# Seven block products for eight in the up projections of a two-layer decoder trunk

## The chip, the cores and the metric

One NeuronCore of a Trainium2 chip runs the whole program. The metric is the device time of one execution in microseconds (us). The engines that matter are TensorE (PE; its weight loads are listed as PEld), VectorE (DVE), ScalarE (ACT), GpSimd (POOL) and SyncE (SP), which issues the loads.

## The reference

The trunk has two layers on 528 tokens (16 meta tokens ahead of 512), of width 1024: a state-space mixer, then differential attention. Behind each mixer stands a gated feed-forward part with a short causal convolution, and this part is what the change touches.

```python
def conv_ffn(h, w_up, conv_w, conv_b, w_down):      # w_up 1024 x 5632, w_down 2816 x 1024
    up = h @ w_up                                    # h: RMS-normalised, with gain
    up_p = jnp.pad(up, ((0, 0), (2, 0), (0, 0)))
    c = conv_b + sum(conv_w[j] * up_p[:, j:j + L] for j in range(3))
    gate, val = jnp.split(c, 2, axis=-1)
    return (jax.nn.silu(gate) * val) @ w_down
```

All arrays are float32.

## The kernel before

**Layout.** Activations lie transposed: channel on the 128 partitions, token along the row. hT holds the residual in 8 channel tiles of 528 tokens. The tokens of a projection are cut into two spans (ALL: 2 x 264 in layer 0; FROM12: 2 x 258 in layer 1), one PSUM bank each.

**Precision.** Each float32 operand is split into a rounded high part and a remainder (wH and wL for weights, hgH and hgL for the input), and three products (high by high, high by low, low by high) are added up in PSUM. The weights come in "units" of 8 k-tiles by 128 columns (1024 elements a partition). load_unit (line 287) has SyncE bring a unit to one of two slots of raw, split_hi (292) has ScalarE write wH, split_lo (299) has GpSimd subtract and write wL. wH and wL have four slots. unit_products (304) issues a unit's 8 x 3 x 2 = 48 matmuls, all of them under line 314.

**Up projection.** The 2816 gate columns and 2816 value columns make 22 pairs (FT = 22) of a gate tile and a value tile: 44 units a layer, 96 matmuls a pair. The gain is applied on the way to hgH and hgL; the row scale rstd is applied afterwards, when VectorE drains the PSUM banks into u (lines 1796, 1797). The sum of squares behind rstd is made by stat_products (line 854), ScalarE takes the root (1391), VectorE the reciprocal (1787). In TensorE's order these statistics stand inside the third unit.

**Convolution.** For each pair VectorE does two tensor_scalar operations, the first taps (1801), and four scalar_tensor_tensor operations, the later taps (1807). ScalarE applies silu to the gate half cg (1402), VectorE multiplies cg by cv (1814). ScalarE then rounds the product into actH (1404), and VectorE writes the remainder actL (1816). A loop of 11 turns with two pairs each drives every engine; the Chain helper (link) puts a semaphore between dependent VectorE operations.

**Down projection.** In layer 0, eight output tiles with three units each again use unit_products, from actH and actL, and VectorE adds the result to hT. In layer 1, down_by_token (line 937) has 24 matmuls of 512 columns for each of the 22 activation tiles and ends in the output norm.

The order within each engine is the order of the code; engines meet only through semaphores.

## Time and profile before

| | us |
|---|---|
| median of 3 runs | 1274.59 (1274.38 to 1275.67) |
| span of the profiled execution | 1273.0 |
| TensorE busy | 1243.4 (98%) |
| VectorE busy | 751.6 (59%) |
| ScalarE busy | 570.7 (45%) |
| GpSimd busy | 607.4 (48%) |
| products of line 314, share of the chain that ended last | 49% |

The span is the time from the first to the last instruction of one execution, on which all rows below were taken. "Busy" is the time in which an engine had at least one instruction recorded. A recorded duration can contain time in which the instruction was held up inside its engine. "Idle before, releaser" names what ended the wait ahead of an instruction.

### The profile page before, as it was taken

What the parts mean: (1) busy time and instruction counts of PE and PEld (TensorE: products, weight loads), DVE (VectorE), ACT (ScalarE), POOL (GpSimd) and SP (SyncE); (2) the same over time, 40 slices, a digit from 0 to 9 for tenths busy, and PEclk for the clock granted to TensorE, in tenths of its full rate; (3) what the DMA queues carried; (4) which work ended last, traced back from release to release, by engine and by line L of the source; (5) the groups of instructions that cost most, each with busy time, mean ns of one, the idle gap of its engine ahead of it and who ended that gap; (6) DMA issues with size and microseconds to landing.
All of it is one profiled execution on the core that took longest, in us unless ns stands there. A gap on an engine that the chain in (4) does not pass through costs nothing.

```text
span 1273.0 us, 26292 instructions
## 1 busy us (share of the span) xinstructions
PE 1243.4 (98%) x10335; PEld 1185.3 (93%) x10335; DVE 751.6 (59%) x1028; ACT 570.7 (45%) x957; POOL 607.4 (48%) x361
## 2 busy tenths in 40 slices
PE   5899999999999999999999999999999999999998
PEld 5888999999999999999998988989999999998886
DVE  8997122688888884111455555553688888882002
ACT  7996543343343432222656656633243333432113
POOL 5433566444444345656654544419544344444431
PEclk9999999999999999999999999999999999999999
DMA  8333332223322333333222112113323333233231
GB/s 174 67 72 82 102 100 84 75 75 99 99 82 87 95 95 91 93 91 112 70 69 65 50 51 68 34 50 100 97 71 97 99 96 86 82 99 99 99 99 66
DMA packets 179498, 108.88 MB, mean 86 GB/s; under 512 B 7100, under 2 KB 173789, under 8 KB 179165
## 3 DMA queue, kind: packets, MB, share of 16 engines
q1 hardware_dynamic: 178997, 107.31, 30.0%
q8 instruction: 51, 0.84, 0.3%
q10 hardware_dynamic: 432, 0.59, 0.1%
q14 instruction: 18, 0.15, 0.0%
HBM read 101.59 MB, written 2.10 MB: 81 GB/s over the span
## 4 chain that ended last, share of the span: by engine, by line
PE 86%; issue 6%; POOL 4%; DVE 2%; ACT 1%; DMA 0%; SPq 0%; POOLq 0%; DVEq 0%; ACTq 0%
PE ps L314 49%; PE ps L987 10%; PE ps L937 10%; PE ps L818 7%; PE ps L1024 2%; PE ps L1094 2%; PE ps L772 1%; POOL acc L2028 1%; PE ps L764 1%; PE ps L1070 1%; POOL sqt L2027 1%; PE ps L1028 0%; PE ps L744 0%; DVE ps L1727 0%; PE ps L711 0%
## 5 line engine op out<-in xcount | busy, mean ns | idle before, releaser
L301 POOL TENSOR_TENSOR wL<-raw,wH 128x1024 fp32r<-128x1024 f32 x182 | 446.9, 2467 | 548.8 <-ACT wH L297 523.0
L314 PE MATMUL ps<-hgH,wH 128*128 128x264 f32 (+1 forms) x1408 | 285.3, 284 | 0.0
L314 PE MATMUL ps<-hgH,wL 128*128 128x264 f32 (+1 forms) x1408 | 285.3, 284 | 0.0
L314 PE MATMUL ps<-hgL,wH 128*128 128x264 f32 (+1 forms) x1408 | 285.0, 284 | 0.0
L297 ACT ACTIVATE wH<-raw 128x1024 fp32r<-128x1024 f32 x182 | 186.4, 1048 | 216.4 <-PE ps L314 79.0
L314 PEld LDWEIGHTS ps<-hgH,wH 128*128 128x128 f32 x1408 | 218.9, 189 | 0.1
L314 PEld LDWEIGHTS ps<-hgL,wH 128*128 128x128 f32 x1408 | 218.4, 189 | 0.0
L314 PEld LDWEIGHTS ps<-hgH,wL 128*128 128x128 f32 x1408 | 217.8, 189 | 0.0
L1402 ACT ACTIVATE cg<-cg 128x528 f32<-128x528 f32 (+1 forms) x44 | 28.2, 640 | 266.7 <-DVE cg L1807 266.7
L1807 DVE SCALAR_TENSOR_TENSOR cg<-u,PV,cg 128x528 f32<-128x528 f32 (+1 forms) x88 | 104.9, 1192 | 13.0 <-DVE cv L1801 6.7
L1801 DVE TENSOR_SCALAR cv<-u,PV 128x528 f32<-128x528 f32 (+1 forms) x44 | 111.3, 2530 | 0.0
L987 PE MATMUL ps<-hgH,wH 128*128 128x264 f32 x384 | 83.2, 298 | 0.0
L987 PE MATMUL ps<-hgH,wL 128*128 128x264 f32 x384 | 78.2, 285 | 0.0
L987 PE MATMUL ps<-hgL,wH 128*128 128x264 f32 x384 | 77.9, 284 | 0.0
L314 PE MATMUL ps<-actH,wL 128*128 128x264 f32 x352 | 71.2, 283 | 0.0
L314 PE MATMUL ps<-actH,wH 128*128 128x264 f32 x352 | 71.2, 283 | 0.0
L314 PE MATMUL ps<-actL,wH 128*128 128x264 f32 x352 | 71.2, 283 | 0.0
L1807 DVE SCALAR_TENSOR_TENSOR cv<-u,PV,cv 128x528 f32<-128x528 f32 (+1 forms) x88 | 66.2, 752 | 0.0
L1829 DVE TENSOR_TENSOR ytok<-ps,fgain 128x512 f32<-128x512 f32 x4 | 2.8, 692 | 103.2 <-ACT ysq L1421 103.2
L1465 ACT ACTIVATE Pb<-ps,tiny 128x144 f32<-128x144 f32 (+4 forms) x66 | 34.8, 532 | 63.2 <-DVE tiny L1855 63.1
L987 PEld LDWEIGHTS ps<-hgH,wH 128*128 128x128 f32 x384 | 59.3, 189 | 3.9 <-issue 3.8
L1763 DVE SCALAR_TENSOR_TENSOR hgL<-hT,PV,hgH (+1 forms) x24 | 34.9, 1455 | 43.2 <-ACT hgH L1373 43.2
(301 smaller groups left out, 2384.8 us busy)
## 6 DMA issues: line engine op xcount, KB each, us to landing
raw<-ffn_w_up SPq DMA_DIRECT2D x88, 512.0 KB, 3.8
raw<-ffn_w_down SPq DMA_DIRECT2D x38, 512.0 KB, 3.6
raw<-attn_w_qkv SPq DMA_DIRECT2D x24, 512.0 KB, 3.7
raw<-s_w_glu SPq DMA_DIRECT2D x16, 512.0 KB, 4.0
TT<-KD SPq DMA_DIRECT2D x64, 64.0 KB, 2.4
raw<-attn_w_o SPq DMA_DIRECT2D x8, 512.0 KB, 4.1
raw<-ffn_w_down SPq DMA_DIRECT2D x8, 384.0 KB, 3.4
xb<-x SPq DMA_DIRECT2D x8, 256.0 KB
```

The lines of the kernel that those rows point to most:

```text
L297: nc.scalar.activation(wH[:, slot, 0:nk], raw[:, slot % 2, 0:nk], ACT.Copy).then_inc(w_hi, 1)
L301: nc.gpsimd.tensor_tensor(wL[:, slot, 0:nk], raw[:, slot % 2, 0:nk], wH[:, slot, 0:nk].bitcast(F32), ALU.subtract).then_inc(w_lo, 1)
L314: mm = nc.tensor.matmul(ps[:, bank + b, 0:tw], w[:, slot, k0 + k, :], x[:, kt, t0:t0 + tw], start=first and k == 0 and s0, stop=last and k ...
L818: mm = nc.tensor.matmul(ps[:, bank + b, 0:tw], w[:, n % 4, k, :], x[:, k, t0:t0 + tw], start=k == 0 and s0, stop=k == 7 and s1)
L937: mm = nc.tensor.matmul(ps[:, 2 * t + c, :], x[:, kt, tok], w[:, n % 4, 4 * c:4 * c + 4], start=False, stop=last and w is ws[-1] and x is ...
L987: mm = nc.tensor.matmul(ps[:, unit_bank(n) + b, 0:tw], w[:, n % 4, k, :], x[:, k, t0:t0 + tw], start=k == 0 and s0, stop=k == 7 and s1)
L1024: return nc.tensor.matmul(ps_row[:, base[c] + a:base[c] + b], q[half[c], q0:nk], k[half[c], a:b], start=True, stop=stop)
L1402: nc.scalar.activation(cg[:, t0:], cg[:, t0:], ACT.Silu).then_inc(silu_set[l], 1)
L1465: ins = nc.scalar.activation(Pb[:, c, 0:nk], score_row(i, c), ACT.Exp, bias=mn[:, c:c + 1], scale=-1.0, accum_out=esum[:, c:c + 1])
L1763: V.scalar_tensor_tensor(hgL[:, ds(ct, 1)], hT[:, ds(ct, 1)], PV[:, ds(gain, 1)], hgH[:, ds(ct, 1)].bitcast(F32), ALU.mult, ALU.subtract). ...
L1801: ins = V.tensor_scalar(c[k][:, t0:], u[:, k, 2 + t0:2 + L], col(i, CONV_W + (3 * l + 2) * 2 * FT + k * FT + q), col(i, CONV_B + l * 2 * F ...
L1807: ins = V.scalar_tensor_tensor(c[k][:, t0:], u[:, k, t0 + j:L + j], col(i, CONV_W + (3 * l + j) * 2 * FT + k * FT + q), c[k][:, t0:], ALU. ...
```

## The change

The first 3 pairs of each layer (PLAIN) stay as they are. The other 19 (FAST) are done by Strassen's scheme in its form with seven products. For a pair, the weights are a 2 x 2 block matrix: gate or value columns by the first or second four k-tiles. The input is a 2 x 2 block matrix too: first or second four k-tiles by the first or second token span. Each of the seven products has 4 k-tiles by 3 terms, 12 matmuls over one span. Three of the seven use weight blocks as they are: P1 and P2 the two halves of the gate tile, which are split together (AA), and P4 the last quarter (A22). The other four use sums of blocks (S1 to S4).

- **Input factors.** VectorE makes the normalised input in float32 (normed: 16 half-width operations, rstd now ahead of the product) and four differences (factors). ScalarE rounds the seven factors, and three remainders are made on VectorE, four on GpSimd.
- **Weights.** A pair's raw tiles come in one of two places, raw and the new raw2. VectorE makes four sums a pair of 512 elements a partition (sums_31, sum_2, sum_4). ScalarE rounds, GpSimd makes the remainders: 1024 (AA), 512 (S4), 1024 (S23), 512 (S1), 512 (A22).
- **PSUM.** Three banks a pair. ScalarE takes snapshots of the running sum after P1, P6 and P5; VectorE adds three quarters of the result (top_left, bottom_right, bottom_left) from a snapshot and a bank, and ScalarE copies the fourth.
- **Order.** P3 and P4 of pair s are issued among the products of pair s + 1. All of it is unrolled.
- **Convolution.** The first taps go to ScalarE (tap); the later taps and the multiplication stay on VectorE. The product is kept in float32 (act32), and the 22 roundings and remainders (tile_high, tile_low) come behind the last fast pair, beside the start of the down projection. The last two products of pair 18 stand inside the down projection's start.
- **Last quarter.** A22 is split ahead of its use, into a slot of its own for even and odd s.
- fgain's load moves from ScalarE's queue to SyncE's, the clearing of acc behind the last multiplication, ytok and ysq to other places.

```diff
+PLAIN = 3
+FAST = FT - PLAIN
...
+def product_places():
+    order = []
+    for s in range(FAST):
+        order += [("P1", s), ("P2", s)] + ([("P3", s - 1)] if s else []) + [("P6", s), ("P7", s)]
+        order += ([("P4", s - 1)] if s else []) + [("P5", s)]
+    order += [("P3", FAST - 1), ("P4", FAST - 1)]
+    return {p: i for i, p in enumerate(order)}
...
+RING = {"AA": (4, 2), "S23": (6, 2), "S1": (0, 1), "S4": (1, 1), "A22": (2, 1)}
+F_B11, F_B21, F_T2, F_T3, F_T1, F_B22, F_T4 = range(7)
...
+                def product(name, s, weights, part, f, bank, first):
+                    e = WGT[weights, s]
+                    pe.wait_ge(f_hi, len(WGT) * l + e + 1)
+                    pe.wait_ge(f_lo, len(WGT) * l + e + 1)
+                    at = ring(l, weights, s).start + part
+                    xH, xL = FB[:, high_at(f), :, 0:width], FB[:, low_at(f), :, 0:width]
+                    for k in range(4):
+                        for i, (w, x) in enumerate(((wHB, xH), (wHB, xL), (wLB, xH))):
+                            mm = nc.tensor.matmul(ps[:, bank, 0:width], w[:, at, k, :], x[:, k], start=first and k == 0 and i == 0,
+                                                  stop=k == 3 and i == 2, skip_group_check=True)
+                    mm.then_inc(f_used, 1)
...
+                def fast(s):
+                    y, w, z = free_banks(s)
+                    if s == 0:
+                        pe.wait_ge(fb_hi, 7 * l + F_B11 + 1)
+                        pe.wait_ge(fb_lo_pool, 4 * l + 1)
+                    product("P1", s, "AA", 0, F_B11, y, True)
+                    if s == 0:
+                        pe.wait_ge(fb_hi, 7 * l + F_B21 + 1)
+                        pe.wait_ge(fb_lo_pool, 4 * l + 2)
+                    product("P2", s, "AA", 1, F_B21, w, True)
+                    if s:
+                        third(s - 1)
+                    pe.wait_ge(snap1, FAST * l + s + 1)
+                    if s == 0:
+                        pe.wait_ge(fb_lo_dve, 3 * l + 1)
+                    product("P6", s, "S23", 0, F_T2, y, False)
+                    if s == 0:
+                        pe.wait_ge(fb_lo_dve, 3 * l + 2)
+                    product("P7", s, "S23", 1, F_T3, z, True)
+                    if s:
+                        fourth(s - 1)
+                    pe.wait_ge(snap2, FAST * l + s + 1)
+                    if s == 0:
+                        pe.wait_ge(fb_lo_dve, 3 * l + 3)
+                    product("P5", s, "S1", 0, F_T1, y, False)
...
+                def tap(p, c, done):
+                    col = lambda k: PV[:, k + c * FT + p:k + c * FT + p + 1]
+                    if p > 1:
+                        act.wait_ge(act_set, FT * l + p - 1)
+                    nc.scalar.activation(conv_pair(p)[c][:, t0:], u_pair(p)[:, c, 2 + t0:2 + L], ACT.Identity,
+                                         bias=col(CONV_B + l * 2 * FT),
+                                         scale=col(CONV_W + (3 * l + 2) * 2 * FT)).then_inc(done, 1)
...
+                plain_taps(0)
+                direct_top(0)
+                factor_high(F_B11, 4)
+                factor_high(F_B21, 8)
+                factor_high(F_T2, 11)
+                factor_high(F_T3, 10)
+                factor_high(F_T1, 9)
+                factor_high(F_B22, 8)
+                factor_high(F_T4, 12)
+                plain_taps(1)
+                sums_23(0)
+                sum_1(0)
+                direct_last(0)
+                silu(0)
+                for s in range(FAST):
+                    more = s + 1 < FAST
+                    if s:
+                        third_snap(s - 1)
+                        sum_1(s)
+                        direct_last(s)
+                    first_snap(s)
+                    if more:
+                        direct_top(s + 1)
+                    else:
+                        tile_high(0)
+                    if s < 2:
+                        silu(s + 1)
+                    if s == 0:
+                        plain_taps(2)
+                    sum_4(s)
+                    if not more:
+                        tile_high(1)
+                    if s:
+                        gate_out(s - 1)
+                    if not more:
+                        down_high(0, "P2")
+                    second_snap(s)
+                    if more:
+                        sums_23(s + 1)
+                    else:
+                        tile_high(2)
+                    if not more:
+                        down_high(1, "P7")
+                        tile_high(3)
+                    if s:
+                        silu(PLAIN + s - 1)
+                        val_out(s - 1)
+                third_snap(FAST - 1)
...
+                def normed(ct):
+                    h = span(hT[:, ct], spans)
+                    gain = GAIN_FFN + 8 * l + ct
+                    second = FBf[:, 0, ct, 0:width] if ct < 4 else FBf[:, low_at(F_B22), ct - 4, 0:width]
+                    first = FBf[:, low_at(F_B11 if ct < 4 else F_B21), ct % 4, 0:width]
+                    scales = span(rstd, spans)
+                    V.scalar_tensor_tensor(first, h[:, 0], PV[:, gain:gain + 1], scales[:, 0], ALU.mult, ALU.mult)
+                    V.scalar_tensor_tensor(second, h[:, 1], PV[:, gain:gain + 1], scales[:, 1], ALU.mult,
+                                           ALU.mult).then_inc(fb_set, 1)
+                def factors():
+                    b12 = FBf[:, 0, :, 0:width]
+                    dve.wait_ge(fb_set, 12 * l + 8)
+                    V.tensor_tensor(factor(F_T1), b12, factor(F_B11), ALU.subtract).then_inc(fb_set, 1)
+                    V.tensor_tensor(factor(F_T3), factor(F_B22), b12, ALU.subtract).then_inc(fb_set, 1)
+                    dve.wait_ge(fb_set, 12 * l + 9)
+                    V.tensor_tensor(factor(F_T2), factor(F_B22), factor(F_T1), ALU.subtract).then_inc(fb_set, 1)
+                    dve.wait_ge(fb_set, 12 * l + 11)
+                    V.tensor_tensor(factor(F_T4), factor(F_B21), factor(F_T2), ALU.subtract).then_inc(fb_set, 1)
...
+                def sums_31(s):
+                    gate, val = pair_raw(s, 0), pair_raw(s, 1)
+                    for c in range(2):
+                        dve.wait_ge(pair_in[2 * (s % 2) + c], pair_count(l, s))
+                    if s:
+                        dve.wait_ge(f_lo, len(WGT) * l + WGT["S23", s - 1] + 1)
+                    V.tensor_tensor(Wsum[:, 1], gate[:, 0:4], val[:, 0:4], ALU.subtract).then_inc(wsum_set, 1)
+                    V.tensor_tensor(val[:, 0:4], val[:, 0:4], val[:, 4:8], ALU.add).then_inc(wsum_set, 1)
...
+                def top_left(s):
+                    dve.wait_ge(f_used, len(PROD) * l + PROD["P2", s] + 1)
+                    dve.wait_ge(snap1, FAST * l + s + 1)
+                    V.tensor_tensor(quarter(PLAIN + s, 0, 0, spans), snap[:, 0, 0:width], ps[:, chain_bank(s) + 1, 0:width],
+                                    ALU.add).then_inc(c11_set, 1)
...
+                drain(0)
+                for ct in range(CT):
+                    normed(ct)
+                factors()
+                drain(1)
+                sums_31(0)
+                sum_2(0)
+                factor_low(F_T2)
+                factor_low(F_T3)
+                factor_low(F_T1)
+                n = plain_taps(0, 1)
+                sum_4(0)
+                after(n)
+                n = plain_taps(0, 0)
+                after(n)
+                multiply(0)
+                drain(2)
+                for s in range(FAST):
+                    more = s + 1 < FAST
+                    if s:
+                        bottom_right(s - 1)
+                    if more:
+                        sums_31(s + 1)
+                    n = plain_taps(s + 1, 1) if s < 2 else val_tap_1(s - 2)
+                    if more:
+                        sum_2(s + 1)
+                    else:
+                        tile_low(0)
+                    if s < 2:
+                        after(n)
+                        last = plain_taps(s + 1, 0)
+                        after(last)
+                    else:
+                        last = val_tap_0(s - 2, n)
+                    top_left(s)
+                    if more:
+                        sum_4(s + 1)
+                    else:
+                        tile_low(1)
+                    if s:
+                        n = gate_tap_1(s - 1)
+                    after(last)
+                    multiply(PLAIN + s - 2)
+                    if s:
+                        gate_tap_0(s - 1, n)
+                        if not more:
+                            tile_low(2)
+                        bottom_left(s - 1)
+                bottom_right(FAST - 1)
...
+                def weight_low(name, s):
+                    pool.wait_ge(f_hi, len(WGT) * l + WGT[name, s] + 1)
+                    at = ring(l, name, s)
+                    V.tensor_tensor(wLB[:, at], weight_source(name, s), wHB[:, at].bitcast(F32),
+                                    ALU.subtract).then_inc(f_lo, 1)
...
+                for j in range(4, 2 * PLAIN):
+                    split_lo(pool, nu + j, (nu + j) % 4)
+                weight_low("AA", 0)
+                factor_low(F_B11, 9)
+                factor_low(F_B21, 12)
+                weight_low("S23", 0)
+                factor_low(F_B22, 11)
+                weight_low("S1", 0)
+                weight_low("A22", 0)
+                factor_low(F_T4, 12)
+                for s in range(1, FAST):
+                    weight_low("AA", s)
+                    weight_low("S4", s - 1)
+                    weight_low("S23", s)
+                    weight_low("S1", s)
+                    weight_low("A22", s)
+                weight_low("S4", FAST - 1)
```

## Rows read from the trace of the kernel before

**Rows 1.** The page: TensorE's busy time, span, count; granted clock by slice.

```profile
PE 1243.4 (98%) x10335; PEld 1185.3 (93%) x10335; DVE 751.6 (59%) x1028; ACT 570.7 (45%) x957; POOL 607.4 (48%) x361
...
PEclk9999999999999999999999999999999999999999
```

**Rows 2.** Chain that ended last: start us, us, what.

```profile
232.69 373.09 PE ps L314 x3060
605.78 6.60 PE ps L987 x54
...
900.63 240.77 PE ps L314 x2004
```

**Rows 3.** Windows, line 314 alone: stretch, us, PE busy (x), PEld, clock, DMA.

```profile
260.00:460.00 200.00, 200.00 (x1637) 200.00 (x1636) 1.00 0.31 90
920.00:1120.00 200.00, 200.00 (x1667) 200.00 (x1667) 1.00 0.32 93
```

**Rows 4.** Timeline of VectorE, 216 to 262 us: start, duration, instruction.

```profile
233.46 3.45 DVE L1787 RECIPROCAL rstd<-sqt 128x528 f32<-128x528 f32 x1 [8.76 <-ACT sqt L1391]
...
247.59 0.70 DVE L1797 TENSOR_TENSOR u<-ps,rstd 128x528 f32<-128x528 f32 x1
...
259.54 0.55 DVE L1801 TENSOR_SCALAR cg<-u,PV 128x528 f32<-128x528 f32 x1 [0.19 <-DVE u L1797]
260.01 2.63 DVE L1801 TENSOR_SCALAR cv<-u,PV 128x528 f32<-128x528 f32 x1
```

**Rows 5.** Timeline of GpSimd, the same stretch.

```profile
235.88 4.75 POOL L301 TENSOR_TENSOR wL<-raw,wH 128x1024 fp32r<-128x1024 f32 x2 [2.59 <-ACT wH L297]
247.22 4.94 POOL L301 TENSOR_TENSOR wL<-raw,wH 128x1024 fp32r<-128x1024 f32 x2 [6.58 <-ACT wH L297]
259.69 2.66 POOL L301 TENSOR_TENSOR wL<-raw,wH 128x1024 fp32r<-128x1024 f32 x1 [7.53 <-ACT wH L297]
```

**Rows 6.** Timeline of VectorE, 300 to 324 us.

```profile
309.12 2.67 DVE L1807 SCALAR_TENSOR_TENSOR cg<-u,PV,cg 128x528 f32<-128x528 f32 x1 [0.15 <-DVE cv L1801]
...
312.61 0.77 DVE L1807 SCALAR_TENSOR_TENSOR cg<-u,PV,cg 128x528 f32<-128x528 f32 x1
313.30 0.76 DVE L1807 SCALAR_TENSOR_TENSOR cv<-u,PV,cv 128x528 f32<-128x528 f32 x1
```

**Rows 7.** Timeline of GpSimd, 300 to 324 us.

```profile
306.01 5.21 POOL L301 TENSOR_TENSOR wL<-raw,wH 128x1024 fp32r<-128x1024 f32 x2 [7.53 <-ACT wH L297]
```

**Rows 8.** Groups by form: xcount, busy us, mean ns, idle before.

```profile
L301 POOL TENSOR_TENSOR wL<-raw,wH 128x1024 fp32r<-128x1024 f32 x176 | 435.9, 2489 | 535.5 <-ACT wH L297 509.7 <-PE ps L744 16.4 <-DVE Ab L1866 7.3
...
L297 ACT ACTIVATE wH<-raw 128x1024 fp32r<-128x1024 f32 x176 | 181.5, 1055 | 192.7 <-PE ps L937 73.2 <-PE ps L314 55.2 <-PE ps L818 23.9
...
L1814 DVE TENSOR_TENSOR cg<-cg,cv 128x528 f32<-128x528 f32 x22 | 15.6, 709 | 2.7
...
L1402 ACT ACTIVATE cg<-cg 128x528 f32<-128x528 f32 x22 | 14.2, 646 | 134.2 <-DVE cg L1807 134.2
...
L1663 DVE TENSOR_TENSOR E<-E,tmpE 128x1024 f32<-128x1024 f32 x8 | 9.7, 1218 | 0.2
...
L551 POOL TENSOR_TENSOR F1b<-P,Bst 128x512 f32<-128x512 f32 x6 | 6.5, 1109 | 21.7 <-PE ps L744 21.7
...
L1946 DVE TENSOR_TENSOR hT<-hT,ps 128x258 f32<-128x258 f32 x16 | 6.0, 411 | 3.1 <-PE ps L1136 3.1
...
L1385 ACT ACTIVATE cg<-ps,PV 128x528 f32<-128x528 f32 x8 | 5.6, 695 | 0.0
```

**Rows 9.** Instructions on tile u, layer 0: duration ns min/median/max.

```profile
L1807 DVE SCALAR_TENSOR_TENSOR cg<-u,PV,cg x44: 767/769/2673, 241.5 to 485.8; 128x528 f32<-128x528 f32 x44
...
L1801 DVE TENSOR_SCALAR cv<-u,PV x22: 542/2628/2648, 240.8 to 481.4; 128x528 f32<-128x528 f32 x22
```

**Rows 10.** Windows, TensorE alone: stretch, us, busy (x), granted clock, DMA.

```profile
20.00:30.00 10.00, 4.90 (x23) 1.00 0.97 198
30.00:40.00 10.00, 6.33 (x109) 0.84 0.35 72
```

More of the change, by code:

```diff
@@ L176, in build @@
         rstd = at("rstd", [P, L], F32)
+        O_ACC = top[0]
         acc = at("acc", [P, L], F32)
@@ L1783, in ffn, with step, drain @@
                 nu, nd = (U_UP0, U_DN0) if l == 0 else (U_UP1, U_DN1)
+                width = spans[0][1]
+                weight = lambda p, c, j: PV[:, CONV_W + (3 * l + j) * 2 * FT + c * FT + p:][:, 0:1]
+                steps = [0]
+                def step(ins):
+                    ins.then_inc(conv_step, 1)
+                    steps[0] += 1
+                    return steps[0]
+                def drain(p):
+                    dve.wait_ge(w_used, nu + 2 * p + 2)
+                    bank = 4 * (1 - p % 2)
+                    for c in range(2):
+                        ins = V.tensor_tensor(span(u_pair(p)[:, c, 2:2 + L], spans), pspan(bank // 2 + c, spans),
+                                              span(rstd, spans), ALU.mult)
+                    ins.then_inc(up_free[l], 1)
@@ L1819, in ffn @@
+                tile_low(11)
+                n = val_tap_1(FAST - 1)
+                tile_low(12)
+                n = val_tap_0(FAST - 1, n)
+                tile_low(13)
+                after(n)
+                multiply(FT - 1)
+                for kt in range(14, FT):
+                    tile_low(kt)
                 if l == 0:
```

538 lines of the change are left out of this document (413 added, 125 removed).

## The prediction

> **What bounds the kernel now.** I read the page first: TensorE is busy for 1243.4 us of the 1273.0 us span, at full clock in every slice [rows 1]. The chain of work that ended last says the same of the two up phases: from 232.69 us one unbroken piece of 373.09 us (the layer 0 up and down projections), from 900.63 us one of 240.77 us (the layer 1 up projections) [rows 2]. Inside them the windows give 200 us for 1637 products of 264 columns, 122.2 ns each, and 200 us for 1667 of 258 columns, 120.0 ns each [rows 3]. So an up pair of 96 products costs 11.73 us (layer 0) or 11.52 us (layer 1), and fewer products would be a gain as long as nothing else becomes slower than they are. That "nothing else" is what I looked at next, in the timelines of VectorE and GpSimd.
>
> **A resource no busy share shows.** At 259.69 us GpSimd runs one weight split of 2.66 us, to 262.35. VectorE's tensor_scalar that starts at 260.01 takes 2.63 us, to 262.64 [rows 4, 5]; alone the same form takes 542 ns [rows 9]. The scalar_tensor_tensor at 309.12 takes 2.67 us, to 311.79, where its neighbours take 0.77, and GpSimd's two splits end at 311.22 [rows 6, 7]. Over layer 0 this form goes from 767 to 2673 ns [rows 9]. But the multiplication u<-ps,rstd at 247.59, one operand in PSUM, takes its ordinary 0.70 us in the middle of two splits [rows 4, 5]. I read this as exclusion: a VectorE operation with both tensor inputs in SBUF, and a GpSimd one that reads SBUF, never run together; the second waits for the end of the first. It acts both ways: VectorE's op of 259.54 ends at 260.09, and the split recorded as 2.66 us ends 2.26 us after that, so 2.26 us is its true hold. VectorE's op then ends 0.29 us (tensor_scalar) or 0.57 us (scalar_tensor_tensor) after the split. Today a pair asks for two splits, 4.5 us, and some 5 us of VectorE: under 11.73, so it costs nothing.
>
> **The change, part by part.** Products: seven of four k-tiles by three terms are 84 per fast pair for 96. It saves 12 x 122.2 = 1.47 us in layer 0, 1.44 in layer 1; over 19 + 19 pairs 55.2 us. A fast pair is 10.26 us of TensorE (10.08 in layer 1). This is the whole gain, and the best case is 1274.6 - 55 = 1219.
>
> GpSimd per fast pair: two splits of 1024 columns (AA, S23), three of 512 (S1, A22, S4), 3584 columns for 2048. Holds: 2 x 2.26, and for 512 columns 1.14 (half of it; the 512-column form on GpSimd records 1.11 [rows 8]): 7.9 us. By recorded times, 2 x 2.49 and 3 x 1.25, 8.7 us.
>
> VectorE per fast pair, both inputs in SBUF: four weight sums, four later taps, one multiplication, nine operations. Shortest each: 0.55 to 0.57, as behind a split, 5.0 us; back to back 0.69 for a tap (312.61 to 313.30) [rows 6] and an estimated 0.62 for the rest (0.71 recorded, less the 0.08 by which two taps overlap), 5.9 us; by recorded times 0.71 and 0.77 [rows 8, 9], 6.6 us. The three bank sums read one PSUM operand, about 0.41 each [rows 8], and may run beside GpSimd. The first taps go to ScalarE, which frees VectorE of the two tensor_scalars.
>
> So the exclusive work per fast pair is 7.9 + 5.0 = 12.9 us at the least and 8.7 + 6.6 = 15.3 us at the most, against 10.26 us of TensorE. Both ends are above the 11.73 us of today. I take 14.3 us, nearer the upper end, because the order leaves moments with neither holder: after the fourth weight sum VectorE waits for ScalarE to split S4, copy C12 and do the gate tap (about 0.55 + 0.4 + 0.65 = 1.6 us from the rows of ScalarE [rows 8]), and S23's GpSimd split also waits behind these in ScalarE's queue; VectorE's next sums wait for that split. Pairs 1 to 18 of both layers, against the mean of 11.73 and 11.52: 36 x (14.3 - 11.62) = +96 us.
>
> The Trainium skill, SBUF — State Buffer, section "Who interferes with whom", names this as one read interface shared by VectorE and GpSimd, held for the whole instruction, with the loser fully blocked, for two-SBUF-input operations as well. Read to the letter, with every instruction holding for its whole recorded time, it would make the pair 15.3 us and the kernel 1274.6 + 132 + 44 + 17 = 1468. By that rule the trace agrees on who blocks whom, but its holds are shorter than the records: 0.57 us behind a split for an operation that records 0.77 alone.
>
> ScalarE per fast pair: weight copies 3584 columns (3.7 us at 1055 ns per 1024), three snaps and one quarter at no more than 0.7, two first taps and a silu of 0.65 [rows 8]: 5.3 to 8.4 us, under 14.3, at nothing while that cover lasts. The table loads at the loop's turns vanish with it. Loads: the same bytes through SP, now a pair at a time two pairs ahead; at nothing, hidden by 10 us per pair. Unrolling: TensorE's straight code already does 54 products in 6.60 us [rows 2], 122.2 ns each as in the loop, so nothing in either direction.
>
> Start of each layer. Time from the reciprocal at 233.46. Today the fourth pair (index 3) ends at 276 products x 0.1222 from 232.69, that is at 32.9. After the change its last product P5 must wait for this exclusive work. GpSimd: two splits (4.75 [rows 5]), AA of pair 3, S23, AA of pair 4 (6.8), four factor lows (about 9.3), S1 and A22 (2.3): 23.1. VectorE: 16 half-width normalised tiles at 0.35 (5.6), four factor differences and three factor lows of 1056 columns at 1.15 (8.1; 1.22 recorded for 1024 [rows 8]), seven weight sums (4.3), seven taps and a product (5.5): 23.5. GpSimd starts at 2.4 [rows 5]; two drains add about 1.3 that nothing covers; then silu of pair 1, pair 2's first taps, S4's copy and the second snap (2.9, since the snap stands behind them on ScalarE). Sum 53, P5 ends at 54.5: +22 us in each layer. With no exclusion the same chain ends near 36, +3 us.
>
> End of each layer. P3 and P4 of the last pair, 24 products, come after the rest, but are in the 84. All activation splits move here: 22 lows of about 0.62, six taps, two multiplications and two bank sums on VectorE, about 19 us, with up to 8.5 us of GpSimd's first down splits. In layer 0 TensorE has 132 + 24 products, 19 us, to hide them: about 8 us uncovered, plus the 2.9 us of P3 and P4 that trail the last period. In layer 1 a tile feeds 24 products of 512 columns, so about 3 + 2.9. Together +17 us.
>
> Sum against the profiled execution's own span: 1273.0 + 96 + 2 x 22 + 17 = 1430. The median of the three timed runs, 1274.6, stands 1.6 us above that span, so the forecast is 1432.
>
> **The rivals.** (A) Exclusion at work, handed over tightly: 12.9 us per pair, start 15 in each layer, ends 14: 1274.6 + 46 + 30 + 14 = 1365. For it: the handovers in the rows are tight. Against: nine waits in a fixed order. (B) The waiting chain rules: 15.5 us or more, start 26 in each layer, ends 20: 1274.6 + 140 + 52 + 20 = 1487. It includes TensorE falling to its lower clock in the gaps: after idle times at 20 to 30 us (4.90 of 10 busy) the next window shows 0.84 [rows 10]. (C) On the other side: TensorE stays the bound, since the exclusion is rarer than I read it. Then 1274.6 - 36 x 1.46 + 2 x 3 + 9 (ends) = 1237. It decides where the exclusive work of a pair is under 10.2 us; the rows give 12.9 at the least, so I give it little. (D) Gain and costs cancel within 0.2% (a kernel like this can hardly be told from no change closer than that), which needs a pair of about 11.2 us with a short start.
>
> **How the numbers follow.** Forecast (13.4 to 15.0 us a pair) 0.62, A 0.15, B 0.13, C 0.08, D 0.02. Predicted 1432. The range of 1350 to 1475 holds the forecast, A down to a still shorter start, and the lower half of B. Faster 0.08, same 0.02, slower 0.90.
>
> **What the profile after would show.** Right: TensorE's busy share in the up phases near 72%, its waits ended by GpSimd's and VectorE's operations; two-SBUF-input operations of VectorE recorded at 1.5 to 3 us beside splits, and none overlapping one for long; a spacing near 14 us between pairs; P5 of the first fast pair some 54 us after the reciprocal. Wrong: TensorE unbroken at 10.3 us a pair, or VectorE's sums and taps at 0.7 us in the middle of GpSimd's splits; a pair over 15.3 us with both engines idle would point to B.

## The result

The changed kernel takes 1476.73 us (median of 4 runs, 1475.57 to 1477.83), the kernel before 1274.73 beside it: a ratio of 1.158, 95% interval 1.156 to 1.160. It is 202 us slower. The forecast was 1432 with a range of 1350 to 1475: the direction and the resource behind it came out as said, the size lies 45 us above the forecast and 1.7 us above the range.

The page of the changed kernel (engine, busy us, share of the span of 1473.8 us, instructions; granted clock in 40 slices), which answers [rows 1]:

```profile
PE 1265.9 (86%) x9879; PEld 1198.6 (81%) x9879; DVE 963.4 (65%) x1177; ACT 706.8 (48%) x1283; POOL 828.3 (56%) x483
...
PEclk9999999688898988999999999999788998879999
```

There are 456 matmuls fewer, and still TensorE is busy for 22 us longer; the clock row, all nines in [rows 1], falls to between six and eight in most slices of the up phases. VectorE gained 212 us of recorded time, GpSimd 221. In the windows of the products' own line, against [rows 3] (columns: stretch, us, PE busy and count, PEld, granted clock, DMA share, GB/s):

```profile
320.00:520.00 200.00, 154.10 (x1092) 151.75 (x1092) 0.89 0.25 69
1060.00:1260.00 200.00, 153.39 (x1092) 150.86 (x1091) 0.88 0.25 69
```

1092 products in 200 us where there were 1637. 84 of them make a pair: 15.4 us a pair for the former 11.7. The chain that ended last was one piece from 900.63 us in [rows 2]; now it is cut in front of the layer 1 down projection (start us, us, what):

```profile
1330.63 2.81 DVE cg L2217
1333.44 2.75 DVE lows L2311
1336.19 0.34 DVE u L2300
1336.54 0.14 issue
1336.67 3.65 PE ps L1162 x16
```

A tap and a remainder at 2.8 us each are on it, each about four times as long as one of them alone (0.76 and 0.7 us).

Cut at the reciprocal behind the row scale (233.46 us before, 234.11 after; in layer 1 901.40 and 1004.92), at the end of the fourth pair and at the end of the last full fast pair, the two spans compare as follows, in us:

| | before | after | difference | forecast |
|---|---|---|---|---|
| layer 0, reciprocal to fourth pair | 32.9 | 54.5 | +21.6 | +22 |
| layer 0, 18 pairs | 211.5 | 274.1 (15.2 each) | +62.6 | +46 |
| layer 0, to the first addition of the down projection | 16.0 | 34.2 | +18.2 | +11 |
| layer 1, reciprocal to fourth pair | 32.4 | 53.8 | +21.4 | +22 |
| layer 1, 18 pairs | 207.6 | 273.7 (15.2 each) | +66.1 | +50 |
| layer 1, to the end of the kernel | 131.6 | 141.3 | +9.7 | +6 |

That is 199.6 of the 200.8 us between the two spans. The starts came as forecast; the pairs brought 33 us more and the ends 11 us more.

**One turn of the loop.** TensorE in layer 0, only its idle times, once a pair (start, us, instruction, idle before and what ended it):

```profile
397.39 0.78 PE L1050 MATMUL ps<-FB,wH 128*128 128x264 f32 x2 [3.37 <-issue]
412.75 0.48 PE L1050 MATMUL ps<-FB,wH 128*128 128x264 f32 x2 [3.64 <-issue]
```

One pair is 412.75 - 397.39 = 15.36 us. The idle time ends just after bottom_left (L2300) has read its bank. That bank is written next by P7; P1 waits for it because the kernel asks for all three banks of a pair ahead of P1. VectorE in this turn (timeline; beside [rows 4, 6]):

```profile
396.76 0.41 DVE L2300 TENSOR_TENSOR u<-snap,ps 128x264 f32<-128x264 f32 x1
398.54 0.43 DVE L2295 TENSOR_TENSOR u<-snap,ps 128x264 f32<-128x264 f32 x1 [1.36 <-ACT snap L1705]
398.89 0.69 DVE L2273 TENSOR_TENSOR Wsum<-raw 128x512 f32<-128x512 f32 x1
399.49 1.77 DVE L2274 TENSOR_TENSOR raw<-raw 128x512 f32<-128x512 f32 x1
401.19 1.79 DVE L2217 SCALAR_TENSOR_TENSOR cgv<-u,PV,cgv 128x528 f32<-128x528 f32 x1
402.90 0.68 DVE L2278 TENSOR_TENSOR Wsum<-raw 128x512 f32<-128x512 f32 x1
403.50 2.91 DVE L2217 SCALAR_TENSOR_TENSOR cgv<-u,PV,cgv 128x528 f32<-128x528 f32 x1
406.34 0.42 DVE L2290 TENSOR_TENSOR u<-snap,ps 128x264 f32<-128x264 f32 x1
406.67 1.45 DVE L2285 TENSOR_TENSOR Wsum<-raw,Wsum 128x512 f32<-128x512 f32 x1
408.04 2.87 DVE L2217 SCALAR_TENSOR_TENSOR cg<-u,PV,cg 128x528 f32<-128x528 f32 x1
410.83 0.70 DVE L2222 TENSOR_TENSOR act<-cgv 128x528 f32<-128x528 f32 x1
411.45 0.76 DVE L2217 SCALAR_TENSOR_TENSOR cg<-u,PV,cg 128x528 f32<-128x528 f32 x1
412.13 0.41 DVE L2300 TENSOR_TENSOR u<-snap,ps 128x264 f32<-128x264 f32 x1
```

GpSimd in the same turn (beside [rows 5, 7]), and then ScalarE's part of it up to the third snapshot, with its gate tap behind the fourth weight sum's copy:

```profile
399.10 3.31 POOL L2640 TENSOR_TENSOR wL<-raw,wH 128x512 fp32r<-128x512 f32 x2 [4.13 <-ACT wH L1648]
403.09 2.75 POOL L2640 TENSOR_TENSOR wL<-raw,wH 128x1024 fp32r<-128x1024 f32 x1 [0.67 <-ACT wH L1648]
405.79 4.55 POOL L2640 TENSOR_TENSOR wL<-Wsum,wH 128x512 fp32r<-128x512 f32 x2
```

```profile
396.87 0.64 ACT L1740 ACTIVATE cgv<-cgv 128x528 f32<-128x528 f32 x1 [4.59 <-DVE cgv L2217]
397.42 0.81 ACT L1712 ACTIVATE cgv<-u,PV 128x528 f32<-128x528 f32 x1
398.14 0.37 ACT L1705 ACTIVATE snap<-ps 128x264 f32<-128x264 f32 x1
...
404.40 0.83 ACT L1712 ACTIVATE cg<-u,PV 128x528 f32<-128x528 f32 x1
```

Read it in two stretches. From 398.89 to 412.13 VectorE has no idle time: its records follow each other, and those beside GpSimd's remainders are 1.45 to 2.91 us long. The tap at 403.50 waits for the remainder that ends at 405.84 and is done at 406.41, 0.57 us later, as in [rows 6, 7]. top_left (L2290), with one operand in PSUM, takes its ordinary 0.42. This stretch, 13.24 us, is the exclusive work of a pair. From 412.13 to the next sum, 2.12 us, neither engine has exclusive work: VectorE drains bottom_left, then idles for 1.36 us. bottom_right waits for the third snapshot, which stands behind the silu and the value tap on ScalarE, and the silu (idle 4.59) waits for VectorE's last gate tap. GpSimd idles for 4.13 us until ScalarE, behind the same snapshot, has copied S1. 13.24 + 2.12 = 15.36, and the turns from 300 to 540 and from 1070 to 1310 us look alike: the stretch is 13.22 to 13.24 us in layer 0 and 13.14 to 13.30 in layer 1, the rest 2.09 to 2.13.

Groups by form (count | busy, mean ns | idle before), against [rows 8], and the later gate taps of the even pairs on tile u, against [rows 9]:

```profile
L2640 POOL TENSOR_TENSOR wL<-Wsum,wH 128x1024 fp32r<-128x1024 f32 x38 | 102.0, 2684 | 12.1 <-ACT wH L1648 10.6
...
L2285 DVE TENSOR_TENSOR Wsum<-raw,Wsum 128x512 f32<-128x512 f32 x38 | 58.4, 1536 | 0.0
L2273 DVE TENSOR_TENSOR Wsum<-raw 128x512 f32<-128x512 f32 x38 | 31.8, 838 | 0.0
```

```profile
L2217 DVE SCALAR_TENSOR_TENSOR cg<-u,PV,cg x22: 754/2329/2905, 265.6 to 560.8; 128x528 f32<-128x528 f32 x22
```

The same form of sum is recorded at 0.84 us on the average where it stands ahead of the remainders and at 1.54 where it stands beside them. The gate tap's median of 769 ns [rows 9] is now 2329 in these pairs.

### The profile page after: what moved, and what is told of

The parts are those of the page before. It is cut to its first block and busy times, and to the rows that moved or that the text cites. A ratio compares the mean times of both kernels' runs of the same rounds, so it can differ in the third digit from the quotient of the medians.

```text
span 1473.8 us, 25204 instructions
## 1 busy us (share of the span) xinstructions
PE 1265.9 (86%) x9879; PEld 1198.6 (81%) x9879; DVE 963.4 (65%) x1177; ACT 706.8 (48%) x1283; POOL 828.3 (56%) x483
## 3 DMA queue, kind: packets, MB, share of 16 engines
q8 instruction: 80, 1.31, 0.4%
## 5 line engine op out<-in xcount | busy, mean ns | idle before, releaser
L1050 PE MATMUL ps<-FB,wH 128*128 128x264 f32 (+1 forms) x2128 | 448.6, 311 | 163.6 <-issue 114.2
L1050 PEld LDWEIGHTS ps<-FB,wH 128*128 128x128 f32 x2128 | 380.1, 217 | 171.5 <-issue 120.4
L373 POOL TENSOR_TENSOR wL<-raw,wH 128x1024 fp32r<-128x1024 f32 (+1 forms) x106 | 255.8, 2417 | 308.2 <-ACT wH L369 282.4
L1050 PE MATMUL ps<-FB,wL 128*128 128x264 f32 (+1 forms) x1064 | 329.0, 309 | 0.0
L2640 POOL TENSOR_TENSOR wL<-raw,wH 128x512 fp32r<-128x512 f32 (+1 forms) x114 | 223.5, 1974 | 173.0 <-ACT wH L1648 173.0
L1050 PEld LDWEIGHTS ps<-FB,wL 128*128 128x128 f32 x1064 | 228.6, 215 | 0.0
L369 ACT ACTIVATE wH<-raw 128x1024 fp32r<-128x1024 f32 (+1 forms) x106 | 110.6, 1045 | 217.3 <-PE ps L1141 93.3
L2640 POOL TENSOR_TENSOR wL<-Wsum,wH 128x1024 fp32r<-128x1024 f32 x76 | 166.0, 2191 | 35.9 <-ACT wH L1648 34.4
L2217 DVE SCALAR_TENSOR_TENSOR cgv<-u,PV,cgv 128x528 f32<-128x528 f32 (+1 forms) x88 | 151.0, 1720 | 7.9 <-ACT cgv L1712 7.9
L1648 ACT ACTIVATE wH<-raw 128x512 fp32r<-128x512 f32 (+1 forms) x114 | 83.6, 766 | 58.4 <-PE ps L1050 58.4
L1141 PEld LDWEIGHTS ps<-act32H,wH 128*128 128x128 f32 x352 | 56.0, 193 | 11.3 <-issue 5.9
```

The source lines that it names most:

```text
L369: nc.scalar.activation(wH[:, slot, 0:nk], raw[:, slot % 2, 0:nk], ACT.Copy).then_inc(w_hi, 1)
L373: nc.gpsimd.tensor_tensor(wL[:, slot, 0:nk], raw[:, slot % 2, 0:nk], wH[:, slot, 0:nk].bitcast(F32), ALU.subtract).then_inc(w_lo, 1)
L1050: mm = nc.tensor.matmul(ps[:, bank, 0:width], w[:, at, k, :], x[:, k], start=first and k == 0 and i == 0, stop=k == 3 and i == 2, skip_gro ...
L1141: mm = nc.tensor.matmul(ps[:, 4 + 2 * (g % 2) + b, 0:tw], w[:, n % 4, k, :], x[:, t0:t0 + tw], start=kt == 0 and s0, stop=kt == FT - 1 and s1)
L1648: nc.scalar.activation(wHB[:, ring(l, name, s)], weight_source(name, s), ACT.Copy).then_inc(f_hi, 1)
L2217: return V.scalar_tensor_tensor(o, u_pair(p)[:, c, t0 + j:L + j], weight(p, c, j), o, ALU.mult, ALU.add)
```

## The experiments

All kernels are the changed kernel with one edit, except where more are named. The edits are shown shortened: a comment in them stands for lines that are left out. A ratio is against the kernel before, run on the same chip (1276.02 us for e1 to e4, 1276.04 for e5 to e8, 1275.09 for e9 and e10). The changed kernel stood beside a kernel before of 1274.73, so a difference from it can be off by 1 or 2 us. "Pairs" is the time of the 18 fast pairs of a layer, cut as above.

### e1: the pairs' weight remainders as fills

```diff
-    V.tensor_tensor(wLB[:, at], weight_source(name, s), wHB[:, at].bitcast(F32), ALU.subtract).then_inc(f_lo, 1)
+    link(V.memset(wLB[:, at].bitcast(F32), 0.0))
+    V.memset(wLB[:, at].bitcast(F32), 0.0).then_inc(f_lo, 1)
```

> Edit: in the changed kernel GpSimd's 95 weight remainders per layer (tensor_tensor, two SBUF reads) become two fills each of the same slot, which read nothing and take about as long together (a fill of 528 columns took 0.54 us, so 1.06 for 512 and 2.1 for 1024, against 1.14 and 2.26). The remainders of the fast pairs are left out of the result. Theory E (a VectorE operation with two SBUF inputs and a GpSimd operation that reads SBUF exclude each other): GpSimd keeps nearly its load, but VectorE's sums and taps go back to 0.69 to 0.77 us, and the fast pair falls from 15.3 us to what VectorE and ScalarE need in their order, 11 to 12 us; the time falls by 36 x 3.8 = 135 us, to 1320 to 1360 us. Rival G (GpSimd's own load of 8 us with its waits is the bound): the pair stays at 14.5 us or more, over 1440 us. Rival C (TensorE's lower clock in the gaps sets the pace): the pair stays above 14 us.

Measured: 1277.92 us in one run. Pairs 183.4 and 182.3 us, 10.2 and 10.1 each; starts 46.5 and 45.8; ends unchanged (34.1 and 141.1). VectorE, one turn:

```profile
332.41 0.68 DVE L2273 TENSOR_TENSOR Wsum<-raw 128x512 f32<-128x512 f32 x1
333.01 0.69 DVE L2274 TENSOR_TENSOR raw<-raw 128x512 f32<-128x512 f32 x1
333.61 0.76 DVE L2217 SCALAR_TENSOR_TENSOR cgv<-u,PV,cgv 128x528 f32<-128x528 f32 x1
...
337.91 0.77 DVE L2217 SCALAR_TENSOR_TENSOR cg<-u,PV,cg 128x528 f32<-128x528 f32 x1 [1.31 <-ACT cg L1712]
```

GpSimd's fills fall beside it (7.0 us of them in a turn), and every sum and tap has its short time. TensorE is the bound again at its 84 products. So GpSimd's reads cost (274.1 + 273.7) - (183.4 + 182.3) = 182 us in the pairs and 16 in the starts. The fills, 7.0 us a turn, are somewhat less work than the 7.9 us of holds that they replace; that the amount isn't what counts, e4 shows, where GpSimd keeps every subtraction. The miss on the size of this run is instructive: I had expected a slower bound to appear behind the exclusion, and none did. The wait for the third snapshot is still there (1.45 us), and the first gate tap now waits for ScalarE's (1.31 us at 337.91, the wait that the prediction had named), but VectorE has time to spare.

### e2: the third snapshot ahead of the silu

```diff
                 for s in range(FAST):
                     if s:
-                        third_snap(s - 1)
                         sum_1(s)
 ...
                     second_snap(s)
+                    third_snap(s)
```

> Edit: on ScalarE the third snap of pair s stands ahead of the silu and the value tap of pair s - 1, not behind them. Same instructions. In the changed kernel's trace VectorE idles 1.70 us in each turn (396.84 to 398.54, from the end of the last gate tap to the bottom-right sum) because that snap waits in ScalarE's queue behind the silu and the value tap. Theory E with this wait as the missing term: the pair falls by 1.2 to 1.7 us, to 13.7 to 14.1 us, and the time by 45 to 60 us, to 1415 to 1432 us. Rival G or C: the wait is cover for something else, and the time moves by less than 10 us.

Measured: 1442.78 us (1441.45 to 1444.32), ratio 1.130 (1.128 to 1.132), 34 us less than the changed kernel. Pairs 258.8 and 256.3. bottom_right now starts right behind bottom_left, so the 1.36 us are gone, but 0.9 us a pair is what they were worth: part of it comes back elsewhere, in front of top_left and the gate tap:

```profile
395.63 0.43 DVE L2289 TENSOR_TENSOR u<-snap,ps 128x264 f32<-128x264 f32 x1 [1.34 <-PE ps L1050]
...
399.30 1.73 DVE L2216 SCALAR_TENSOR_TENSOR cg<-u,PV,cg 128x528 f32<-128x528 f32 x1 [2.64 <-ACT cg L1712]
```

This is a turn with much of it. From 300 to 500 us the gate tap waits for ScalarE's first tap in 12 of 14 turns, 22.1 us in all: the wait behind the fourth weight sum that the prediction had counted on, open only now. Ahead of it, ScalarE's copy of AA waits for the previous pair's P2 (2.31 us at 395.69), and P1 and P2 together take some 4.7 us here for 3.1 us where the clock is full (e9). TensorE's low clock can have a part in what came back; no run separates it.

### e3: TensorE kept busy in its gap

```diff
                 for s in range(FAST):
+                    if s:
+                        keep_busy(24)   # 24 products into the unused bank 3
```

> Edit: ahead of each fast pair but the first TensorE does 24 more products of 264 columns into a bank that nobody reads (2.9 us, inside its gap of 3.65 us), so that its clock has less reason to fall. Nothing is left out. Rival C (the half clock, granted for 3.4 us about twice in 30 us, sets part of the period): the clock stays at 1.0 through the fast pairs, and each pair is 1 to 1.8 us shorter, the time 35 to 65 us less. Theory E: the clock rises, but the cycle runs over VectorE, GpSimd and ScalarE, and TensorE's own speed is in its slack: the pair stays at 15.3 us within 0.3, the time within 12 us of 1477, at most a few us less in the ends of the layers.

Measured: 1473.33 us (1472.09 to 1477.18), ratio 1.156 (1.154 to 1.157). The pair stays at 15.4 us. The granted clock of 320 to 480 us rises from 0.88 to 0.94, not to 1.00, so the low clock was halved and not taken away; but a pair with half as much of it is no shorter. TensorE's clock isn't in the circle of waits of the changed kernel.

### e4: the layer 1 accumulators in PSUM

```diff
-                    o = conv_pair(p)[c][:, t0:]
+                    o = ps[:, 3 + 4 * c, 0:L - t0]      # layer 1, fast pairs but the last three
```

The silu writes its result to SBUF and the multiplication reads that and the value bank. The multiplication moves ahead of top_left, and this in both layers.

> Edit, in layer 1 alone, pairs 3 to 18: the two convolution accumulators lie in the two free PSUM banks and not in SBUF, so that the four later taps and the multiplication have one SBUF input each; the multiplication stands a little earlier on VectorE. Same operations, same sizes, same engines; layer 0 is the control. Theory E: in layer 1 the taps no longer wait for GpSimd's splits; exclusive work falls from 13.8 us to 7.9 + 4 x 0.62 = 10.4 us a pair, and with the waits of the order the pair falls from 15.25 to 11.5 to 13.5 us; 16 pairs, 30 to 60 us; layer 0 stays at 15.4. Rivals G and C: neither an operand's place nor GpSimd's load changes what they name, so layer 1 stays at 15 us or more and the time at 1477 within 5 us.

Measured: 1403.82 us (1395.46 to 1406.64), ratio 1.098 (1.094 to 1.102). Layer 0, where only the multiplication's place changed, has a P1 every 15.5 us and takes 278.3 us for its pairs, 4 us more than in the changed kernel, so the gain doesn't come from that move; layer 1 falls from 273.7 to 207.0 us for its pairs, with 10.6 us for most of the later ones. Windows of either layer (us, PE, PEld, DVE, ACT, POOL busy, clock, DMA share, GB/s):

```profile
320.00:480.00 160.00, 126.75 (x865) 124.95 (x866) 144.70 (x124) 74.21 (x125) 105.25 (x52) 0.85 0.24 67
1120.00:1240.00 120.00, 114.91 (x923) 113.06 (x924) 103.10 (x133) 76.60 (x134) 111.81 (x55) 0.99 0.34 94
```

GpSimd is now 93% busy and TensorE 96%. Taps with one operand in PSUM (two of them in 1.54 us at 1187.18) run in the middle of a remainder recorded from 1186.67 to 1190.77. The exclusion hangs on where the operands lie, not on the engines being busy, and GpSimd's amount of subtractions alone doesn't hold the pair at 15 us.

### e5: all GpSimd reads of the up phases as fills

Besides e1's, the factor remainders, the last plain pair's two splits and the first four down splits of each layer become fills.

> Edit: as in e1_fills, and GpSimd's other remainders in both up phases (the third plain pair's two units, the four input factors, the first four units of the down projection) are pairs of fills as well. These remainders and those of the fast pairs are left out of the result. It asks what the starts and ends of the layers cost once no exclusion is left in them. In e1_fills the start (from the reciprocal to the first product of pair 1) is 46.5 and 45.8 us, the pairs 183.4 and 182.3, the end of layer 0 34.1. My forecast's rival without exclusion says: start near 36, the end of layer 0 near 22. Then the start falls by 10 us in each layer and the ends by some 10 in all, and the time is about 1250 us. If the starts stay above 43 us and the end of layer 0 above 31 us, they are the waiting order's (factors, snaps, taps one after the other) and TensorE's half clock, and the time is 1265 us or more.

Measured: 1241.89 us in one run, 34 us less than the kernel before. Starts 37.8 and 37.3 us, pairs 183.8 and 182.5, ends 22.9 and 134.5. Without the exclusion the seven products do what they promise, within 5 us of the 1237 that the prediction's rival C gave them.

### e6: the remainders of pairs 1 to 18 on VectorE

```diff
-                    weight_low("AA", s)       # and S4, S23, S1, A22: GpSimd
+                    weight_low("S1", s)       # and A22, AA, S4, S23: VectorE, each behind a sum or a tap
```

> Edit: the weight remainders of pairs 1 to 18 are made on VectorE and not on GpSimd, in VectorE's order beside the sums they follow; nothing is left out. VectorE takes about 0.6 us for 512 elements and 1.15 for 1024, GpSimd holds 1.14 and 2.26. Theory E: since the two never work together, only the sum of their times counts, and it falls from 7.9 + 5.9 + 1.3 to 7.1 + 4.1 = 11.2 us; with the waits the pair is 12 to 13.2 us, the time 1365 to 1410 us, although VectorE has 50% more to do. Rival V (VectorE's own load and order set the pace, and GpSimd works beside it): VectorE's added 4.1 us come on top, the pair is 17 us or more, the time over 1520 us.

Measured: 1366.28 us (1363.74 to 1368.53), ratio 1.070 (1.068 to 1.072): 110 us faster than the changed kernel, with GpSimd idle throughout the pairs. Pairs 221.9 and 219.9, 12.3 and 12.2 each. VectorE does a remainder of 1024 columns in 1.22 us where GpSimd takes 2.4 and shuts VectorE out meanwhile. Its own sequence of 11.0 to 11.1 us has one idle time, the 1.2 us in front of bottom_right.

### e7: the last quarter split late

```diff
-        order += [("S1", s), ("A22", s)]
-    order += [("S4", FAST - 1)]
+        order += ([("A22", s - 1)] if s else []) + [("S1", s)]
+    order += [("S4", FAST - 1), ("A22", FAST - 1)]
```

and one slot for it in place of two, ScalarE's and GpSimd's splits of it one turn later.

> Edit: the last part of the change undone alone: the quarter A22 of pair s is split one turn later, ahead of S1 of pair s + 1, into a single slot. It reads the raw tiles, so their place comes free later, and with it the load of pair s + 2. Theory E with the early split as cover: the exclusive work is the same 13.8 us, but the load (about 4 us to landing, two tiles) now stands between GpSimd's split and VectorE's next sums: the pair becomes 18 to 22 us and the time 1575 to 1720 us. Rival H (the loads are hidden, whatever the order, as the exclusive work fills the turn): the time within 12 us of 1477.

Measured: 1539.48 us (1536.27 to 1540.49), ratio 1.206 (1.204 to 1.208). The pair goes to 17.2 us, less than the 18 to 22 expected, and the time stays under the 1575. The wait is the one that was meant: the raw tiles are released by this split, so the next load but one comes late, and VectorE waits for it in 11 of the 12 turns between 300 and 500 us, 32.5 us in all:

```profile
399.89 0.69 DVE L2270 TENSOR_TENSOR Wsum<-raw 128x512 f32<-128x512 f32 x1 [2.33 <-DMA raw<-ffn_w_up]
```

Rival H falls. The early split of the change is worth 2 us a pair, 63 us in all. TensorE's wait for the split itself has no part in it: in the fifth to seventeenth fast pairs its only idle time in a turn stands ahead of P1 (4.3 us in the mean), and none ahead of P4, which reads A22.

### e8: three edits together

e2's snapshot, e4's accumulators in layer 1, and the three remainders of 512 columns on VectorE, with AA and S23 left to GpSimd.

> Edit: e2_snap_first and e4_psum_taps (layer 1) together, and the three remainders of 512 elements (S1, A22, S4) on VectorE; nothing is left out. Theory E, exclusive work per pair: layer 1 two splits 4.5 + four sums 2.5 + three remainders 1.8 = 8.8 us, under TensorE's 10.08, so the pair is 10.1 to 10.8 us; layer 0 4.5 + 5.9 + 1.8 = 12.2 us, so 12.4 to 13.2 us. Time: 1477 - 18 x 2.4 - 18 x 4.7 = 1349, range 1335 to 1365 us; still over the 1275 us of the kernel before, because layer 0 stays above 11.73 us a pair and the starts and ends stay. Rival V: VectorE's 1.8 us more a pair come on top of e4_psum_taps: over 1404 us.

Measured: 1398.43 us (1397.02 to 1403.27), ratio 1.096 (1.094 to 1.099), far above the 1335 to 1365 expected. Layer 0 takes 14.0 us a pair, more than e6's 12.3. In layer 1, 12.5 us a pair, there is a new ring: ScalarE's first gate tap of the next pair waits for the multiplication, and that stands behind a sum which AA's remainder holds up (2.89 us). The waits of 1080 to 1230 us (who waits for whom: us, times, longest):

```profile
ACT ps L1742 <- DVE act L2251: 41.9, 12, 3.5
```

and behind this tap on ScalarE stands the second snapshot, for which TensorE waits 1.3 us. The single bank doesn't by itself ask for this wait: by the code the multiplication reads the silu's result in SBUF and the value bank, and the gate bank was last read by the silu, on ScalarE itself. The edit puts the wait for the multiplication ahead of both taps, where only the value tap needs it; what the run would be with the gate tap free of it is not shown. Gains of single edits don't add up: here the largest remainders stayed on GpSimd, and the accumulators with their new wait close another ring.

### e9: e6 and e2 together

> As e6 (the weight remainders of pairs 1 to 18 on VectorE), and as in e2 the third snapshot of pair s is put right behind the second on ScalarE instead of behind the next silu and value tap. Nothing is left out. In e6 VectorE works without a pause in each turn (11.0 us) except for 1.15 us before bottom_right, which waits for the third snapshot; a pair takes 12.17 us. Theory (VectorE is e6's bound, and the wait on ScalarE's queue is the rest of its pair): 11.1 us a pair, 36 x 1.1 = 40 us less than e6's 1366: about 1326. Rival (the snapshot was only the last of several waits of equal length, TensorE's products or the weight copies come next): 1350 to 1366. Both stay above the 1276 of the kernel before.

Measured: 1354.88 us (1353.96 to 1356.0), ratio 1.063 (1.061 to 1.065), the fastest of the variants that leave nothing out. Pairs 216.0 and 214.1, 12.0 and 11.9 each: the theory (1326) falls, and the rival's 1350 to 1366 holds. The 1.2 us at bottom_right are gone, and almost the same wait stands one instruction later, where VectorE wants ScalarE's copy of S1:

```profile
1152.79 0.42 DVE L2302 TENSOR_TENSOR u<-snap,ps 128x258 f32<-128x258 f32 x1
1154.29 0.69 DVE L2270 TENSOR_TENSOR wL<-raw,wH 128x512 fp32r<-128x512 f32 x1 [1.07 <-ACT wH L1648]
```

That copy stands behind the same silu and value tap. VectorE's own work, 10.8 us, is above TensorE's 10.1 and hardly below the 11.5 of the kernel before: with starts and ends still 68 us longer than before there is nothing to win even with this wait gone.

### e10: the first down splits as fills

> The changed kernel, with GpSimd's four first splits of the down projection in each layer replaced by two fills of the same tile each (no SBUF read); the remainders of those four weight tiles are left out of the computation. Nothing else is touched, the pairs keep their 15.2 us. The time behind the last fast pair was 34.2 us in layer 0 and 141.3 in layer 1 (16.1 and 131.6 before), 28 us more in all. Theory (the part above the forecast 17 is VectorE's taps and remainders held up by these splits): 34.2 falls to 24 to 27 and 141.3 to 135 to 137, the kernel to 1459 to 1465. Rival (it is the bare number of operations on VectorE and ScalarE, the 22 roundings and remainders in a queue with the last taps): no more than 4 us less, 1472 to 1477.

Measured: 1457.44 us (1456.58 to 1458.28), ratio 1.143 (1.141 to 1.145), 19 us less than the changed kernel, a little more than expected, and the pairs are as before (275.3 and 273.0). The ends are 22.9 and 134.6 us for 34.2 and 141.3. TensorE's idle time at the start of the layer 0 down projection, first in the changed kernel, then in e10:

```profile
567.04 0.48 PE L1141 MATMUL ps<-act32H,wH 128*128 128x264 f32 x2 [4.33 <-DVE u L2300]
582.73 0.48 PE L1141 MATMUL ps<-act32H,wH 128*128 128x264 f32 x2 [2.22 <-DVE lows L2311]
```

```profile
566.35 0.48 PE L1141 MATMUL ps<-act32H,wH 128*128 128x264 f32 x2 [0.21 <-DVE lows L2311]
577.85 0.48 PE L1141 MATMUL ps<-act32H,wH 128*128 128x264 f32 x2 [1.28 <-DVE lows L2311]
```

The two first down splits held VectorE's gate tap (560.80, 2.90 us) and a remainder (563.62, 2.85) ahead of bottom_left. 18 of the ends' 28 us are these four splits a layer.

## Why the prediction came out as it did

**The bound and the resource.** Right. VectorE's operations with both tensor inputs in SBUF and GpSimd's reads of SBUF exclude each other; e1 puts fills in place of the reads and the pair falls to TensorE's 10.2 us; e4 keeps the reads, moves VectorE's accumulators to PSUM, and most later pairs take 10.6. Rival C falls: it is what the kernel would do without the exclusion (e5, 1241.89 for its 1237). D falls with it. A (12.9 us, tight) falls at 15.2. One row doesn't fit my wording: the tensor_scalar of [rows 4] (2.63 us) reads one tensor, u, and its other inputs are one value a partition, so "both tensor inputs in SBUF" doesn't cover it, and it was held all the same. The changed kernel has no such operation in its pairs, and no run here tests it.

**The saving in products.** Right: e1's pairs are 53.4 us shorter than those of the kernel before, for 36 x 1.46 = 52.6.

**The pair, the step that failed.** I took 14.3 us, of which 12.9 were the least sum of holds and 1.4 a wait. The sum of holds was nearly right: 13.24 us measured. The wait was mis-sized and put in the wrong place: 2.12 us for 1.4. I expected VectorE to wait behind the fourth weight sum for ScalarE's copies and gate tap. In the changed kernel it hardly does (0.7 us once in the 13 turns from 300 to 500 us): ScalarE's gate tap is done at 405.23, and VectorE, held up by GpSimd, comes for it at 408.04. That wait is open only with the holds away (e1) or the snapshot moved (e2). The dead stretch is around bottom_left and bottom_right instead, where ScalarE's order (last gate tap, silu, value tap, third snapshot) closes the ring. 1.36 us of it are that wait; the other 0.76 are the two bank sums, which I had put beside GpSimd and so at nothing, while GpSimd idles there. In the mean of both layers 15.22 us were measured against 14.3, and 36 x 0.92 is the 33 us. I had listed what stands in ScalarE's queue for the start of a layer, and didn't walk the same queue once around the steady turn. e2 shows what the snapshot's place is worth: 33 us in the pairs. That e2's pair is then 14.3 us, the forecast's number, is partly luck.

In part this is what rival B said (a waiting chain, 15.5 us or more). By the prediction's own sign, a pair over 15.3 us with both engines idle, the steady turn of layer 0 (15.36) points to B, and B's 1487 is 10 us from the measured time where the forecast is 45 away. But B had 26 us for each start (21.5 measured) and 20 for the ends (28 measured), and it counted on TensorE's low clock, for which e3, taking half of it away, finds no part. The truth lies between the two.

**The starts.** Right in size: 54.5 and 53.8 us to the end of the first fast pair, for 54.5. Right in kind, too: with all reads of GpSimd taken away 37.8 and 37.3 remain (e5; I had said near 36). Of the 16.6 us between, e1 puts 8.0 on the weight remainders, and e5 the rest on the factor remainders and the plain pair's splits together.

**The ends, the second term.** Forecast +17, measured +28. In layer 0 I had TensorE's 156 products hide all but 8 us of VectorE's 19 and GpSimd's 8.5. Cover does not add up like that: P3, P4 and each activation tile want their operand at a place in the order, and a hold just ahead of bottom_left stops TensorE for 4.3 us, whatever is left to do behind it. In layer 1, 3 + 2.9 us were forecast and 9.7 came. e10 assigns 11.3 and 6.7 us to the first down splits; where the other 10 us come from is not shown.

**Nothing from ScalarE and the loads.** ScalarE's amount of work, 75.59 of 160 us or 7.3 us a pair, is under the cover as forecast; its order is not, as told. The loads were right for the change as made: none is waited for in its steady turns. e7 shows how near it was: with the raw tiles released one turn later the load is waited for in nearly each.

**The rule and the rows.** The Trainium skill, SBUF — State Buffer, section "Who interferes with whom", says that a VectorE instruction with two SBUF inputs contends with a GpSimd one that reads SBUF, and not with one that only writes it. The changed kernel's turn bears out the first half (sums of up to 1.77 us beside remainders), e1 the second (0.69 us beside fills). Read with whole recorded times it would have given 15.3 us a pair and 1468 us, close to the measured 15.2 and 1477, but by luck: the holds sum to 13.24 us, and the rest is the dead stretch, which is no hold.

## What to carry to other kernels

Where operations of two engines shut each other out, sum up what both hold in one turn as if it were an engine of its own, and compare that sum with the bound before spending VectorE or GpSimd work on fewer matmuls; then walk each in-order queue once around the turn, because the ring of waits comes on top of the sum. Where the sum is above the bound, work given to GpSimd is not off VectorE's hands: doing it on VectorE itself was 110 us faster here, accumulators in PSUM took a quarter off the pairs of their layer, and a load, split or snapshot that is hidden in one place of the order isn't in another.

## What the runs showed of the hardware

- The exclusion in numbers: a remainder of 1024 columns takes GpSimd some 2.4 us (2.40 at 396.83 in e2, with VectorE idle) and a VectorE operation that comes meanwhile is recorded at up to 2.91 us, ending 0.57 us after it. Two fills in its place, 1.9 us of GpSimd, cost VectorE nothing (0.69 us a sum).
- For this subtraction VectorE (1.22 us for 1024 columns) is twice as fast as GpSimd (2.40 us).
- TensorE's clock: with one idle time of 3.4 to 3.7 us in nearly each 15.4 us the granted clock was 0.88 in the mean (320 to 480 us); in e6, with 1.8 to 1.9 us ahead of some pairs and 0.3 ahead of the others, 0.95 (320 to 480 us) and 0.93 (1020 to 1200 us); in e9, with 1.6 us ahead of each pair, 1.00 in both. The low level coincided with the longer gaps. In the changed kernel it cost nothing measurable, as far as e3 could take it away.
